# A two-block transformer on one core: token-wise and feature-wise eviction of the turned input behind two norms

## The reference

```python
# first block (gated / mixing)
mixed = jnp.concatenate([o_diff.astype(x.dtype), o_mlstm], axis=-1) @ w_out[l]
x = x + rmsnorm(mixed, norm_mix_post[l])
h = rmsnorm(x, norm_mlp_pre[l])
u = jnp.square(jax.nn.relu(h @ w_up[l]))            # 1024 -> 4096
x = x + rmsnorm(u @ w_down[l], norm_mlp_post[l])    # 4096 -> 1024
# second block, first layer
hn = rmsnorm_2(x, attn_norm[i])
x = x + mixer_dilated(hn, a_w_qkv[j], ...)          # qkv = hn @ w_qkv, 1024 -> 3*3*1024
```

## Time and profile before

| what | us |
|---|---|
| three runs, median (lowest to highest) | 1104.12 (1103.91 to 1104.41) |
| the profiled execution | 1104.38 |
| its span (first to last instruction) | 1102.6 |
| PE busy | 1088.1 of the span |
| DVE, ACT, POOL busy | 774.9, 642.0, 23.0 |

### The profile page before, as it was taken

How to read it: one execution, slowest core, us unless ns; L and a number is a source line. 1 busy time by engine, 2 the same in 40 slices (tenths; PEclk the granted TensorE clock), 3 DMA queues, 4 the chain that set the end, 5 groups by cost and what they waited for, 6 DMA issues and landing times.

```text
span 1102.6 us, 19200 instructions
## 1 busy us (share of the span) xinstructions
PE 1088.1 (99%) x7052; PEld 950.0 (86%) x7052; DVE 774.9 (70%) x1405; ACT 642.0 (58%) x1112; POOL 23.0 (2%) x55
## 2 busy tenths in 40 slices
PE   9999999999999999999999999999999999999998
PEld 8967798999878887888888999999877779999997
DVE  5876655555567667666755977877876748877876
ACT  5476655445465656566566555555666656555553
POOL 0000000000000000100010000000001010000000
PEclk9999999999999999999999999999999999999999
DMA  8643446656646554365524565565552425656562
GB/s 320 188 134 96 153 143 203 189 189 181 189 123 205 180 175 131 97 191 186 169 67 153 170 194 190 172 199 193 163 188 84 146 97 171 194 188 194 174 203 96
DMA packets 117038, 184.15 MB, mean 167 GB/s; under 512 B 6640, under 2 KB 70384, under 8 KB 116720
## 3 DMA queue, kind: packets, MB, share of 16 engines
q1 hardware_dynamic: 116688, 183.03, 52.3%
q10 hardware_dynamic: 288, 0.29, 0.1%
HBM read 182.25 MB, written 1.05 MB: 166 GB/s over the span
## 4 chain that ended last, share of the span: by engine, by line
PE 86%; DVE 6%; ACT 5%; issue 1%; DMA 1%; SPq 0%; DVEq 0%; ACTq 0%
PE ps L673 11%; PE ps L675 10%; PE ps L674 10%; PE ps L697 9%; PE ps L699 9%; PE ps L698 9%; PE ps L756 5%; PE ps L757 5%; PE ps L758 5%; DVE w_lo L1766 3%; PE ps L847 2%; PE ps L870 2%; ACT w_hi L1184 2%; PE ps L890 1%; DVE hid L2262 1%; PE ps L819 1%
## 5 line engine op out<-in xcount | busy, mean ns | idle before, releaser
L1766 DVE TENSOR_TENSOR w_lo<-w_stage,w_hi 128x1024 fp32r<-128x1024 f32 x336 | 403.7, 1222 | 180.9 <-ACT w_hi L1184 179.9
L1184 ACT ACTIVATE w_hi<-w_stage 128x1024 fp32r<-128x1024 f32 x336 | 349.6, 1054 | 185.1 <-PE ps L675 89.4
L697 PE MATMUL ps<-aT_hi,w_hi 128*128 128x256 f32 x992 | 281.5, 284 | 1.4 <-DVE aT_lo L1780 1.0
L699 PE MATMUL ps<-aT_hi,w_lo 128*128 128x256 f32 x992 | 280.7, 283 | 0.0
L698 PE MATMUL ps<-aT_lo,w_hi 128*128 128x256 f32 x992 | 280.7, 283 | 0.0
L673 PE MATMUL ps<-w_hi,aT_hi 128*128 128x512 f32 x480 | 192.2, 400 | 3.7 <-issue 1.2
L697 PEld LDWEIGHTS ps<-aT_hi,w_hi 128*128 128x128 f32 x992 | 190.2, 192 | 3.3 <-issue 1.3
L698 PEld LDWEIGHTS ps<-aT_lo,w_hi 128*128 128x128 f32 x992 | 190.3, 192 | 1.0
L699 PEld LDWEIGHTS ps<-aT_hi,w_lo 128*128 128x128 f32 x992 | 190.2, 192 | 0.0
L675 PE MATMUL ps<-w_hi,aT_lo 128*128 128x512 f32 x480 | 187.4, 390 | 0.0
L674 PE MATMUL ps<-w_lo,aT_hi 128*128 128x512 f32 x480 | 187.0, 390 | 0.0
(11 more groups left out here) (241 smaller groups left out, 1126.2 us busy)
## 6 DMA issues: line engine op xcount, KB each, us to landing
w_stage<-in_ffn_w_up SPq DMA_DIRECT2D x88, 512.0 KB, 4.6
w_stage<-in_a_w_qkv SPq DMA_DIRECT2D x72, 512.0 KB, 4.1
w_stage<-in_ffn_w_down SPq DMA_DIRECT2D x44, 512.0 KB, 3.3
w_stage<-in_w_up SPq DMA_DIRECT2D x32, 512.0 KB, 4.0
w_stage<-in_w_down SPq DMA_DIRECT2D x32, 512.0 KB, 4.2
w_stage<-in_w_in SPq DMA_DIRECT2D x24, 512.0 KB, 4.7
w_stage<-in_b_w_qkv SPq DMA_DIRECT2D x24, 512.0 KB, 4.5
w_stage<-in_w_out SPq DMA_DIRECT2D x8, 512.0 KB, 3.8
```

What stands on the lines that cost most here:

```text
L697: pe.matmul(o, wh, aT_hi[:, k, :], start=(k == 0), stop=False)
L699: last = pe.matmul(o, wl, aT_hi[:, k, :], start=False, stop=(k == KT - 1))
L1184: act.activation(w_hi[:, slot, :], w_in[:, slot, :], ACT.Copy).then_inc(hi_done[slot], 1)
L1766: dve.tensor_tensor(w_lo[:, slot, :], w_in[:, slot, :], w_hi[:, slot, :].bitcast(F32), ALU.subtract).then_inc(lo_done[slot], 1)
```

## The change

Behind the mixing block, token tile 0 is turned into two banks of its own (`turn_first`), evicted at once in pieces of 128x128, and the first half of the up products (features `a0`, `a1`) runs for token tile 0 alone (`pair_cols`, t=0), in place of the 16 idle products. Then token tile 1 is turned in eight pieces, each with its own signal (`turn_second`), over four banks that are used twice, and the same products run for it (t=1). `dense_cols` does the other half as before. The orders of ACT and DVE follow; one quarter's `w_lo` is written by POOL.

Behind the MLP, the turned input is signalled and evicted one feature tile at a time (`turn_fine`, `turned_fine`), and the last four transposes of token tile 1 stand between the first products. `pick_scale` moves one quarter back. One more quarter's `w_lo` is written by POOL.

```diff
+            def pair_cols(stg, n0, names, norm, t):
+                for q in range(2):
+                    slot = await_weights(stg, n0 + q, 0)
+                    for kk in range(4):
+                        k = 4 * q + kk
+                        if t:
+                            pe.wait_ge(*is_drained(st[norm], f"h{k}"))
+                        elif kk == 0:
+                            pe.wait_ge(*is_drained(st[norm], f"e{q}"))
+                        for f in range(2):
...
+                            pe.matmul(o, wh, ah, start=(k == 0), stop=False)
+                            pe.matmul(o, wh, al, start=False, stop=False)
+                            last = pe.matmul(o, wl, ah, start=False, stop=(k == KT - 1))
...
+                    if t and q == 0:
+                        signal(stg, n0 + q, last)
...
+            def turn_second(name, ready, ks):
+                stg = st[name]
+                pe.wait_ge(*ready[1][ks[0] // 4])
+                for k in ks:
+                    b = bank(stg, f"h{k}")
+                    pe.wait_ge(*is_free(stg, f"h{k}"))
+                    pe.transpose(ps[:, b, (k // 4) * P:(k // 4 + 1) * P], x[:, 1, k * P:(k + 1) * P], ident)\
+                        .then_inc(full[b], 1)
...
-            turn_x("norm_mlp", ready, 0, LOW)
-            turn_x("norm_mlp", ready, 0, HIGH)
+            turn_first("norm_mlp", ready, LOW)
+            turn_first("norm_mlp", ready, HIGH)
             last_rows(S_, 4, "r3", 1, range(5, KT))
-            spin(16, ps[:, 7, 0:P], ident)
-            turn_x("norm_mlp", ready, 1, LOW)
-            turn_x("norm_mlp", ready, 1, HIGH)
...
-            dense_cols(S_, 0, 0, A4, "norm_mlp", {1: lambda: spread_scale("norm_mlp")})
+            pair_cols(S_, 0, A4, "norm_mlp", 0)
+            turn_second("norm_mlp", ready, LOW)
+            turn_second("norm_mlp", ready, HIGH)
+            pair_cols(S_, 0, A4, "norm_mlp", 1)
+            dense_cols(S_, 0, 0, A4, None, {2: lambda: spread_scale("norm_mlp")}, skip=(0,))
...
-            turn_x("norm_a", ready, 1, LOW, "in")
-            turn_x("norm_a", ready, 1, HIGH, "in")
+            turn_fine("norm_a", ready, 1, LOW)
...
-                    project_heads(S_, NG, units, "norm_a", {2: lambda: pick_scale("norm_a")})
+                    each = {k: lambda k=k: turn_fine("norm_a", a_ready, 1, [k + 4]) for k in range(4)}
+                    project_heads(S_, NG, units, "norm_a", {3: lambda: pick_scale("norm_a")}, each)
...
@@ ACT, behind the mixing block
             post_square(S_, "r", 1, 0)
-            splits(S_, [4])
+            splits(S_, [4, 5])
+            turned_token(nrm, col("g_mlp"), 0)
+            post_square(S_, "r", 1, 1)
+            post_rstd(post, 1)
+            splits(S_, [6])
+            turned_token(nrm, col("g_mlp"), 1)
+            splits(S_, [7])
...
@@ ACT, behind the MLP
             splits(S_, [1])
-            turned(nrm, col("g_a"), LOW)
-            turned(nrm, col("g_a"), HIGH)
+            turned_fine(nrm, col("g_a"), LOW)
+            turned_fine(nrm, col("g_a"), HIGH)
             splits(S_, [2, 3])
...
@@ POOL
+            split(st["out1"], 5)
+            split(st["mlp_tail"], 0)
...
@@ DVE, behind the MLP
             norm_mean(nrm, 0, 2)
-            splits(S_, [0])
             post_mean(post, 1)
             post_keep(S_, "acc", gain, 1, 1)
             post_add(post, S_, "acc", 1)
-            turned(nrm, col("g_a"), LOW)
+            turned_fine(nrm, col("g_a"), range(2))
             splits(S_, [1])
-            turned(nrm, col("g_a"), HIGH)
+            turned_fine(nrm, col("g_a"), range(2, 4))
+            turned_fine(nrm, col("g_a"), HIGH)
             splits(S_, [2, 3])
             norm_mean(nrm, 1, 4)
```

More of the change, by code:

```diff
@@ L209, in norm_stage, with fine_stage @@
     return Stage(name, uses=uses, counts={"hiT": 8, "mh": 4, "ms": 2, "rstd": 2, "ln_norm": 2, **more})
+def fine_stage(name, banks, scale, first=(), **more):
+    uses = [(f"e{j}", b) for j, b in enumerate(first)] + [(f"h{k}", banks[k % 4]) for k in range(8)] + [("scale", scale)]
+    return Stage(name, uses=uses, counts={"hiT": 16 if first else 8, "mh": 4, "ms": 2, "rstd": 2, "ln_norm": 2, **more})
 def turn_stage(name, **more):
@@ L656, in signal, with dense_rows @@
                     ins_.then_inc(used[by[0][1]], 1)
-            def dense_rows(stg, i, n0, names, turned=None, tiles=range(KT), after=None, of=(aT_hi, aT_lo), ready=None):
+            def dense_rows(stg, i, n0, names, turned=None, tiles=range(KT), after=None, of=(aT_hi, aT_lo), ready=None,
+                           each=None):
                 for k in tiles:
@@ L679, in dense_rows, with dense_cols @@
                         signal(stg, n0 + q, last)
+                    if each and k in each:
+                        each[k]()
                     if kk == 1 and after and q in after:
                         after[q]()
-            def dense_cols(stg, i, n0, names, turned=None, after=None, order=BY_PAIRS):
+            def pair_cols(stg, n0, names, norm, t):
[8 more added lines that the diff above has]
+                        for f in range(2):
+                            c0 = kk * 2 * P + f * P
+                            wh, wl = (w[:, slot, c0:c0 + P] for w in (w_hi, w_lo))
+                            o = ps[:, bank(stg, names[f]), t * P:(t + 1) * P]
+                            if k == 0 and t == 0:
+                                pe.wait_ge(*is_free(stg, names[f], 0))
+                            ah, al = (a[:, k, t * P:(t + 1) * P] for a in (aT_hi, aT_lo))
+                            pe.matmul(o, wh, ah, start=(k == 0), stop=False)
+                            pe.matmul(o, wh, al, start=False, stop=False)
+                            last = pe.matmul(o, wl, ah, start=False, stop=(k == KT - 1))
+                            if k == KT - 1 and t:
+                                last.then_inc(full[bank(stg, names[f])], 1)
+                    if t and q == 0:
+                        signal(stg, n0 + q, last)
+            def dense_cols(stg, i, n0, names, turned=None, after=None, order=BY_PAIRS, skip=()):
                 for q, (pair, deep) in enumerate(order):
+                    if pair in skip:
+                        continue
                     slot = await_weights(stg, n0 + q, i)
@@ L1728, in _, with split @@
                                    u32[:, j * 512:(j + 1) * 512], ALU.mult).then_inc(s["mqk"], 1)
+            def split(stg, n):
+                slot = plan.slot(stg, n)
+                pool.wait_ge(hi_done[slot], plan.turn(stg, n, 0, SLOTS) + 1)
+                pool.tensor_tensor(w_lo[:, slot, :], w_in[:, slot, :], w_hi[:, slot, :].bitcast(F32),
+                                   ALU.subtract).then_inc(lo_done[slot], 1)
+            split(st["out1"], 5)
+            split(st["mlp_tail"], 0)
             def wide_parts(stg, units):
```

91 lines of the change are left out of this document (71 added, 20 removed).

## The result

| | before | changed kernel |
|---|---|---|
| median of 4 runs, us | 1104.15 (1103.91 to 1104.41) | 1112.96 (1112.79 to 1114.63) |
| profiled execution: time, span, us | 1104.38, 1102.6 | 1113.08, 1111.1 |
| mean granted clock of TensorE | 1.000 | 0.997 |
| ratio of the medians | | 1.0078, 95% interval 1.0067 to 1.0090 |

The account below looks back on a forecast made before the run. The prediction took TensorE, busy 99% at full clock, as the bound: what it issues and where it stands still. +0.2 and +5.9 made +6.1 us on 1104.38, 1110.5 profiled, 1110.2 median; range 1106.0 to 1121.5, the forecast's own 1108 to 1113.

Parts of the forecast that it names:

- a rival with a chance of 0.09: TensorE's granted clock falls in a new stall, at either place, costing 2 us: 1112 to 1114; chance 0.09.
- First place: Behind the mixing block: 96 products of 128 columns, a wait and a turn take 13.0 against 12.84, +0.2 us.
- the open chain: Behind the mixing block, token tile 1's transposes and evictions between the two product halves stand uncovered: 2.2 us.
- the first product's wait: Behind the mixing block, the first narrow product waits for token tile 0's evictions until 131.03: 0.22 us.
- the wide one: Narrow fp32r products cost as much as plain f32, 0.223 each: first place +11.0, in all 1121.0; chance 0.18.
- the column pace: Columns, not weight loads, set narrow products' pace, 0.068 each: first place -3.8, in all 1106.2; chance 0.08.
- Second place: Behind the MLP and into the query projection: four terms, 0.36 + 0.7 + 2.95 + 1.9, sum +5.9 us.
- Term 1: Behind the MLP, POOL's subtraction holds DVE's single-column mean until about 320.95 instead of 319.77: +1.2 us.
- Term 2: Behind the MLP, the first product comes 1.49 after the first transpose, not 2.33: -0.84; four inserted transposes cost +0.7.
- Term 3: Query projection: the last transpose's eviction precedes quarter 2's split on ACT, so product 4 waits: +2.95 us, TensorE idle.
- Term 4: Query projection: with the scale picked one quarter later, DVE's three queued `w_lo` wait for it: +1.9 us.
- The rival that was not slower: Narrow products at column pace and DVE not held by POOL: -3.8 and +4.3, +0.5 in all; chance 0.05.

Follow-up runs that it names:

- the last experiment: Second quarter of up products 256 wide, only the first in 128-column halves, against the reordered kernel with token tile 1 turned over six banks: 1100.99 us.
- the kernel without stalls: Changed kernel with scale pick behind quarter 2, MLP tail `w_lo` on DVE, quarter 2's split ahead of the last four evictions, these spread between other work: 1104.04 us.
- stalls filled: Changed kernel plus idle products in both stalls behind the MLP, 12 behind the last inserted transpose and 7 behind the scale: 1109.97 us.
- second place alone: Changed kernel with only the change behind the MLP kept and the old code put back behind the mixing block: 1114.61 us, ratio 1.0092.
- scale early: Changed kernel with the scale picked behind quarter 2 again instead of behind quarter 3: 1111.33 us, ratio 1.0057.
- `w_lo` on DVE: Changed kernel with the subtraction for the MLP's last tail quarter on DVE again, ahead of the mean, not on POOL: 1111.99 us, ratio 1.0067.
- one of the experiments: Changed kernel with the split of quarter 2 ahead of the evictions of the last four transposes on ACT and DVE: 1108.92 us.

## Why the prediction was right, and where its size was off

The terms of the sum came out as foretold, within 0.25 us each: 5.6 us together, where 6.1 was forecast. The rest of the 8.8 us is a fall of the clock at both stalls, which the prediction had as a rival with a chance of 0.09. The 1112.96 lies in the 1112 to 1114 of that rival and, by 0.04, in the 1108 to 1113 that the forecast gave itself. Without the falls the time would have been about 1110, inside the range as well; that it stayed inside with them is owed to the width that the open price of narrow products had given the range, and not to any term for the clock.

**First place, forecast +0.2, measured +0.03.** The parts hold: 0.11 per narrow product was taken and 0.112 measured, 2.2 for the open chain and 2.02, 0.22 for the first product's wait and 0.09. The price had been the widest of the open terms (0.068 to 0.223). Both price rivals are out, the wide one and the column pace; so is the estimate of 7.8 for 96 products by the Trainium skill's back-to-back figure ("TensorE: Matmul & The Clock Gate", Back-to-back issue gap), where 10.76 were measured. Its LDWEIGHTS rule, 107 ns for 128 columns, is within 5% of the 0.112. That the load sets this pace is argued from the nearness of the one-column records (0.101) and of the 256-wide products (0.122); no run here changed the loads alone. What the prediction did not price is the cover: it took 48 products as hiding a norm that had let the transposes start at 135.10 before; in the changed kernel that norm was over at 133.34, and the 48 products ran until 135.80. The 2.4 us that the last experiment won lay there.

**Second place, forecast +5.9.** Term 1, DVE held by POOL: +1.2 forecast, +1.13 measured, and shown by putting the subtraction back (1.12). Term 2, the first product: -0.84 and -0.87; the four inserted transposes 0.7 forecast, 0.46 in the kernel without stalls. Here the step was mis-sized: it took 0.10 for each transpose and 0.08 for each restart behind it, and what a transpose and its restart add is 0.12 together. Term 3, the last transpose and quarter 2: +2.95 forecast; the transpose at 329.22 and product 4 at 332.26 are 3.04 apart, and the stall went with the order on ACT and DVE. (The parts that the prediction adds up for it make 3.16 to 3.21, not its 3.1.) Term 4, the scale: +1.9 and +1.84, and the wait went with the one number. Without the clock the sum of the rows is 5.6, and 5.7 by the run times (stalls filled), where 6.1 was forecast. The upper end of 6.5 that the prediction gives this place does not follow from its bounds: with the +1.35 of term 1 it would be 6.05.

**What was off: the clock.** The prediction held it as a rival of its own, at 2 us a fall (1112 to 1114, where the time lies) and with a chance of 0.09, in place of the forecast. It is not another way for the kernel to go: the stalls of the forecast bring it about, and filling them took it away. It came at both stalls, for 1.68 and 1.6. The forecast should have carried, for each stall that it foretold, the price of a fall times how likely that was. Worked out afterwards, with both it is 1110.2 + 3.3 = 1113.5, and less the 0.5 by which the other terms came out smaller (5.6 for 6.1) it is the 1113.0 that was measured. The price itself was right within 0.4, a stretch of slow products costing half of itself, but the rival counted one such stretch where there were two. The reason given for the small chance, that 2.95 us of stall has no row in the trace of before, was true; that speaks for a wide bound, and not for the case in which nothing happens. The one row that the prediction had for the price, the start of the run, is less plain than it was read: the idle records there pass at half pace, but the granted clock of that stretch is shown as 1.00.

```profile
2.00:4.00 2.00, 2.00 (x11) 2.00 (x11) 0.00 (x0) 0.95 (x1) 0.05 (x2) 1.00 0.72 248
```

The columns are the window, its length, the busy time of PE, PEld, DVE, ACT and POOL, then PEclk, the DMA share and GB/s.

**The rival that was not slower** had no part that came true. It needed 0.063 per narrow product and a DVE that is not held.

**What stays open.** Of how long a gap the clock falls behind, the profiled runs say this much: behind the 2.77 us it fell in four of four (changed kernel, second place alone, scale early, `w_lo` on DVE); behind the 1.70 in two of four; behind the 1.48 with 0.80 close after it in two of five; behind 0.36 with 0.80 in none of four. These are single profiled runs, and what decides in the middle cases they do not tell. The kernel before has clocks of 0.998 too, in 2 of 13, 5 of 21 and 4 of 9 runs, at 1105.4 to 1105.9; where it falls there no profile shows.

## What to carry to other kernels

When work is cut finer so that it starts sooner, the pieces that come late stand in front of something in every in-order queue that evicts them: look at each of those queues for the instruction behind the last piece, and put what is needed next ahead of it. Work that only covers a wait should be no longer than the wait, the more so when it costs more per unit than what it replaces: 24 narrow products did here what 48 had, for 2.4 us less. And a stall that one foretells on TensorE should be priced with the slow stretch behind it.

## What the runs showed of the hardware that was not expected

- An fp32r product of 128 columns that loads its own 128x128 weights takes 0.112 us in a stream, one of 256 columns 0.12, one of 512 0.229: halving the width from 256 to 128 saves next to nothing.
- VectorE and GpSimd can hold each other in both directions. At the second place DVE's one-column instruction took 1.64 us while POOL's subtraction of 128x1024 ran in 2.35; so it is, at 1.62 to 1.64, in all five profiles that have this subtraction. At the first place DVE's own subtraction was already under way, with 0.64 left (127.49 + 1.22, POOL from 128.07), and there POOL's took 0.55 longer, 2.89 or 2.90 in all nine profiles that have it. That the second is a hold is read from these times; no run moved DVE's subtraction away.

```profile
128.07 2.90 POOL L1823 TENSOR_TENSOR w_lo<-w_stage,w_hi 128x1024 fp32r<-128x1024 f32 x1 [63.59 <-ACT w_hi L1255]
```

- A fall of the granted clock behind these stalls cost 1.5 to 1.7 us, about 3.5 us of products at half pace, whether the gap in front of it was 2.77, 1.70 or the pair of 1.48 and 0.80. So with one kernel and one chip whole runs differ by this step: 1107.59, 1108.79 and 1109.05, 1110.42 are the four of one of the experiments.
- At the second place of the kernel before, the only rows of a gap (0.36 and 1.01) are at full clock; filling a gap of 2.77 with idle products kept the clock at 1.00 and took no time of its own: product 4 came 3.03 behind the last transpose, 3.04 without them.
